# Splitting the first activation tiles in another order, and two unused product groups fewer, in a hybrid attention/SSD layer

## The reference, cut to what matters

```python
h = rms_norm(x, norm_gain[i])                 # x: 1024 x 1024
proj = h @ w_in[i]
q, k, v, z_a, z_s, xbc, dt_raw, gate_pre = jnp.split(proj, offsets, axis=-1)
# attention over q, k, v;  SSD over xbc, dt;  gates;  two projections, merge, output projection
x = x + merged @ w_out[i]
```

## Time and profile before

| | |
|---|---|
| median of 3 runs | 1331.56 us (1331.45 to 1332.23) |
| profiled execution, its own time | 1331.9 us |
| its span in the trace | 1330.1 us |
| PE busy | 1322.8 us, 99% of the span |
| DVE, ACT, POOL busy | 865.2, 638.9, 567.4 us |
| granted PE clock, mean | 1.00 of full speed |

### The profile page before, as it was taken

The page is one execution under the profiler, slowest core; times in us unless marked ns, Lnnn a source line. Parts: engine busy times, 40 slices in busy tenths (PEclk is TensorE's granted clock), DMA queues, the critical chain, the costliest instruction groups (busy, mean ns, idle before and its releaser), DMA issues.

```text
span 1330.1 us, 20357 instructions
## 1 busy us (share of the span) xinstructions
PE 1322.8 (99%) x7018; PEld 1061.8 (80%) x7018; DVE 865.2 (65%) x1051; ACT 638.9 (48%) x1194; POOL 567.4 (43%) x340
## 2 busy tenths in 40 slices
PE   8999999999999999999999999999999999999999
PEld 7878777888888888778788787887888878788887
DVE  7858767766776423567576676665756554377897
ACT  7565354554454333545365364552657554522331
POOL 5644564554454454344233343343145545344300
PEclk9999999999999999999999999999999999999999
DMA  7434564434333322766646666466485455523615
GB/s 221 179 103 131 145 164 145 136 104 126 95 109 112 126 95 89 273 211 203 222 147 221 222 200 221 173 205 224 142 312 213 150 194 198 208 96 142 225 45 190
DMA packets 124608, 223.28 MB, mean 168 GB/s; under 512 B 7650, under 2 KB 84194, under 8 KB 121235
## 3 DMA queue, kind: packets, MB, share of 16 engines
q1 hardware_dynamic: 59586, 174.22, 39.2%
q10 hardware_dynamic: 64880, 48.37, 11.4%
q0 software_dynamic: 96, 0.13, 0.0%
HBM read 154.15 MB, written 63.31 MB: 163 GB/s over the span
## 4 chain that ended last, share of the span: by engine, by line
PE 96%; DVE 1%; DMA 1%; SPq 1%; ACT 1%; issue 0%; DVEq 0%
PE F L199 38%; PE F L1119 37%; PE M L2270 4%; PE M L1322 2%; PE M L1366 2%; PE F L2270 2%; PE F L1360 1%; PE F L1336 1%; PE F L1353 1%; PE F L1063 1%; PE M L1360 1%; PE M L1353 1%; PE F L2224 1%; DMA sb_early<-x 1%; PE M L1315 1%; PE M L1347 1%
## 5 line engine op out<-in xcount | busy, mean ns | idle before, releaser
L1119 PE MATMUL F<-sb_tv,sb_whl 128*128 128x512 f32 x1200 | 287.9, 395 | 0.0
L199 PE MATMUL F<-sb_xb,sb_whl 128*128 128x512 f32 x1152 | 282.9, 402 | 0.0
L1119 PEld LDWEIGHTS F<-sb_tv,sb_whl 128*128 128x128 f32 x1200 | 224.9, 187 | 55.1
L199 PEld LDWEIGHTS F<-sb_xb,sb_whl 128*128 128x128 f32 x1152 | 214.1, 188 | 57.0 <-issue 8.1
L199 PE MATMUL F<-sb_X,sb_whl 128*128 128x512 f32 x1080 | 253.0, 395 | 0.0
L199 PEld LDWEIGHTS F<-sb_X,sb_whl 128*128 128x128 f32 x1080 | 202.3, 187 | 50.1 <-issue 0.5
L482 POOL TENSOR_TENSOR sb_whl<-sb_acc,sb_whl 128x512 fp32r<-128x512 f32 x123 | 172.7, 1412 | 156.6 <-ACT sb_whl L556 156.6
L211 POOL TENSOR_TENSOR sb_whl<-sb_wst,sb_whl 128x1024 fp32r<-128x1024 f32 x50 | 125.8, 2515 | 223.8 <-ACT sb_whl L208 223.7
L1119 PE MATMUL F<-sb_xb,sb_whl 128*128 128x512 f32 x900 | 219.7, 396 | 0.0
L1119 PEld LDWEIGHTS F<-sb_xb,sb_whl 128*128 128x128 f32 x900 | 168.2, 187 | 44.4 <-issue 2.2
L556 ACT ACTIVATE sb_whl<-sb_acc 128x512 fp32r<-128x512 f32 x123 | 76.0, 627 | 98.7 <-PE F L1119 82.0
(11 more groups left out here) (248 smaller groups left out, 1823.3 us busy)
## 6 DMA issues: line engine op xcount, KB each, us to landing
sb_wst<-w_units SPq DMA_DIRECT2D x52, 512.0 KB, 5.2
sb_acc<-cs_d SPq DMA_DIRECT2D x8, 2048.0 KB, 7.2
sb_wst<-w_units SPq DMA_DIRECT2D x14, 1024.0 KB, 4.8
sb_acc<-w_units SPq DMA_DIRECT2D x12, 1024.0 KB, 5.1
x_d<-sb_res ACTq DMA_DIRECT2D x24, 512.0 KB, 3.2
sb_early<-x_d SPq DMA_DIRECT2D x8, 1024.0 KB, 6.3
sb_acc<-ecs_d SPq DMA_DIRECT2D x16, 512.0 KB, 8.2
g_d<-sb_res ACTq DMA_DIRECT2D x16, 512.0 KB, 6.1
```

What stands on the lines that cost most here:

```text
L199: last = nc.tensor.matmul(bank, weight(slot, wp, k), act(ap, k, half), start=(k == 0 and wp == 0 and ap == 0), stop=(k == NK - 1 and wp == 1))
L1119: last = nc.tensor.matmul(F[:, BANK[what], :], ring(idx, wp)[:, k * P:(k + 1) * P], moving(what, ap, k), start=(idx < 4 and k == 0 and wp ...
```

## The change

On ACT, `x_high(0)` moves ahead of `square_x(2)`, `b12_copy(0)` moves behind the high part of v_0, and the high part of dt goes away. On POOL, the high part of dt is new, ahead of the low parts. On DVE, `x_low(0)` moves ahead of `norm_x(2)`. On PE, one of the two first unused products and all four ahead of the vdt products go away; the waits follow the producers.

```diff
@@ POOL
+            pool.wait_ge(v_in1, 32)
+            nc.gpsimd.tensor_copy(vw[:, 0, :, 2 * P:VD], dtraw[:]).then_inc(pads_set, 1)
             pool.wait_ge(v_hi, 1)
             v_low(0)
             pool.wait_ge(dt_lo, 1)
             v_low(1)
-            pool.wait_ge(v_hi, 2)
+            pool.wait_ge(pads_set, 3)
             nc.gpsimd.tensor_tensor(vw[:, 1, :, 2 * P:VD], dtraw[:], vw[:, 0, :, 2 * P:VD].bitcast(f32), ALU.subtract).then_inc(dt_lo, 1)
@@ ACT
             square_x(0)
             square_x(1)
+            x_high(0)
             square_x(2)
-            x_high(0)
             x_high(1)
-            b12_copy(0)
             act.wait_ge(v_in1, 32)
             nc.scalar.activation(v_part(0, 0), raw_v(0), ACT.Copy).then_inc(v_hi, 1)
-            nc.scalar.activation(vw[:, 0, :, 2 * P:VD], dtraw[:], ACT.Copy).then_inc(v_hi, 1)
+            b12_copy(0)
             square_x(3)
@@ DVE
             norm_x(1)
+            x_low(0)
             norm_x(2)
-            x_low(0)
             dve.wait_ge(v_in1, 32)
             nc.vector.tensor_copy(v_part(0, 1), raw_v(1)).then_inc(dt_lo, 1)
             x_low(1)
@@ PE
-            unused_products(2, zpad[:, 0:P], zpad[:])
+            unused_products(1, zpad[:, 0:P], zpad[:])
@@ PE
             transpose_x(0)
             transpose_x(1)
-            unused_products(4, C('ones'), C('ident', 0, 2 * P))
-            pe.wait_ge(v_hi, 2)
+            pe.wait_ge(v_hi, 1)
+            pe.wait_ge(pads_set, 3)
             pe.wait_ge(dt_lo, 1)
```

## The result

The changed kernel takes 1333.72 us (median of 20 runs, 1332.76 to 1334.44) against 1331.53 us (20 runs, 1331.38 to 1332.84): ratio 1.0015, 95% interval 1.0009 to 1.0021, 2.2 us slower. The forecast of 1331.7 us was wrong, and the range of 1330.7 to 1333.4 too short by 0.3 us.

What follows compares the result with a forecast made beforehand. Early pace was set by x tile 3's DMA at 16.01 us, then ACT and DVE, with PE only from 29.54. Terms 0 + 0 + 0.05 + about 0.05 gave 1331.56 + 0.1 = 1331.7 us, range 1330.7 to 1333.4.

Steps and rivals of the forecast that it cites:

- I take it that it does, since nothing here shows a fall: PE ahead of the vdt products: the upper clock level survives a pause of 2.9 us, so no time lost.
- rival 2: PE falls to 1.2 GHz in the pause, slowing the 32 vdt products; 1333.1 or 1336.6 us, chances 0.07 and 0.06.
- recovering form: PE's clock falls in the pause but recovers half way through the vdt products: about +1.5 us, 1333.1, chance 0.07.
- lasting form: PE's clock stays low over all 32 vdt products, taking up to 9.1 us: +5 us, 1336.6, chance 0.06.
- Taking them away gives 0 as long as the vdt products start at about 14.3: PE's four unused products, 11.26 to 13.24, lie wholly in a wait for ACT's dt copy: removal priced 0.
- ACT, POOL and DVE: Reordered early stage: tile 0's high part 0.46 us earlier, tile 1's low part +1.08, POOL copy price 0.
- The start of the vdt products: On PE, DVE's cast of v_1 becomes the last gate: start at 14.37 against 14.32, +0.05 us.
- The slack: Idle margin behind the vdt products, absorbing their +0.05 us later start; some 0.5 us ahead of tile 2's transposes.
- the sum: Unused products 0, POOL 0, vdt start 0.05, high part of tile 3 about 0.05: 0.0 to 0.1 us.
- rival 1: DVE's delay, from tile 1's low part waiting for the pair 0 copy, isn't absorbed: up to +1.1 us, 1332.7, chance 0.12.
- Tile 3 at 16.01: The DMA of x tile 3 lands at 16.01 us and sets the early pace; ACT idles 1.76 us for it.
- -1.25 from below: Bound on the gain: PE's whole idle time from behind 14.32 up to 29.54, 1.25 us.

Runs made afterwards that it cites:

- the run without the four: Kernel before with only the four unused products ahead of the vdt products removed; 1333.20 us, ratio 1.0012.
- the run of the order alone: Changed kernel with both groups of unused products put back (2 and 4), leaving the new order on ACT, DVE and POOL; 1331.94 us, ratio 1.0003.
- half of the filling: Kernel before with two of its four unused products left ahead of the vdt products; median 1331.67 us, ratio 1.0004.

## Why the prediction was wrong

**The step that failed is the clock.** I wrote "I take it that it does, since nothing here shows a fall": the absence of a fall in a trace without such a pause was taken for evidence. The clock's loss was rival 2, with the right cost (the first vdt products at 1.2 GHz) and the right sign (the 32 products over 5 us), and had 0.13 of the chance where it should have had most of it: all three traces of the changed kernel show products at the lower level (6.45, 6.61 and 6.83 us for the 32), and all 20 of its runs (1332.76 and up) are slower than all those 87 of before (1332.56 at most). Its picture was half of what happens. It let PE fall in the pause; that is the trace of the run without the four. In the three traces of the changed kernel the clock had not risen yet when the pause began (422 to 428 ns for the transposes ahead of it, and no fall in the granted clock), and it rose only at about the middle of the vdt products. With the four put back, a clock that was late rose while they ran (3.11 us instead of 1.98), ahead of the vdt products. Its recovering form was priced at 1333.1 and its lasting form at 1336.6; measured was 1333.7, between. The lasting form was priced too high besides: sixteen transposes at 3.63 against twice 1.04 us is a factor of 1.75 and not 2, which makes 7.9 us and not 9.1 of the 4.53. The rule that the prediction cited from the Trainium skill ("TensorE: Matmul & The Clock Gate", Part 1) named the case: by that rule work lifts the clock and idling gives it back. The traces agree in that, with 0.54 of the clock from 14.9 to 18.1 us after a pause of 2.85 us, and in the changed kernel with records of 442 ns up to 19 us, when the vdt products had run since 15.08, and of 297 ns from 19.8 on.

**"Taking them away gives 0 as long as the vdt products start at about 14.3"** was the price of the four products, read from their place in a wait. Their time is free; what they do to the clock is not. Measured: 1.7 us alone.

**ACT, POOL and DVE** came out as worked: in the run of the order alone, high part of tile 0 at 9.88 (9.80 forecast), the cast of v_1 starting at 13.70 (13.63), the low part of tile 1 at 14.71 (14.60), the last norm before the low part of tile 2 ending at 20.08 + 1.28 = 21.36 (21.4). The POOL copy took 0.40 us, inside the bounds of 0 and 0.72.

**The start of the vdt products** was mis-sized: I put 0.06 us between the end of the last producer and PE, as ACT's row had it (14.26 to 14.32). Behind DVE's cast it was 14.64 - (13.70 + 0.69) = 0.25 us. The slack was mis-sized too: ACT's squares waited for a landing at 16.01 in the trace that I took it from, and at 15.67 in that of the order alone, so that ACT wants the high part of tile 2 some 0.3 us earlier. With both, the transposes of tile 2 end when ACT wants them, not 0.4 earlier, and the order costs 0.4 us by the medians instead of the 0.1 of the sum. This is rival 1's time in part; how much of it is the later vdt start and how much the copy of pair 0 is open, as said above.

**"Tile 3 at 16.01"** was right as a pace and wrong as a name. The wait counts the loads of tiles 3 and 4 on one semaphore, so the later of the two set it; with its own, tile 3's square started at 14.02 and 14.15, and tile 4's at 15.98. That the pace lies there held: 0.8 us of earlier vdt start gave nothing.

The bound "-1.25 from below" was never tested by the change. The range failed by its upper end: it took in the recovering clock's middle and not its spread up to 1334.4.

## What to carry to other kernels

Products that nobody reads are not free to remove because they lie in a wait: ask what PE's pause becomes without them, whether the clock has risen when it begins, and what runs behind it. If the trace of before has no such pause, it says nothing on the clock's answer, and the case with the slower products deserves the larger chance. Look at the runs as heaps and at their mean clocks, not at the median alone: half of the filling showed no loss by the median and had it in five runs of eleven. And there is a bound on the other side: six products in place of four bought nothing that can be told.

## What the runs showed of the hardware that I had not expected

- By the granted clock, the level did not fall in the pause but at its end (no record lies in the pause to test it by): in the run without the four it reads 1.00 from 11.5 to 14.2 us, when no product ran, 0.70 from 14.3 to 14.7, and 0.54 from 14.9 to 18.1.
- The point of the rise varies between executions of almost the same start. Four unused products took 1.98 us in one trace and 3.11 in another, though they began at 11.26 in both. With the pause filled, that made no difference to the total that can be told (1331.9 us with the early rise, 1331.63 with the late one).
- The granted clock reads 1.00 ahead of the first recorded change, even where records of 421 to 442 ns show the lower level. Durations of one shape tell it; the column doesn't.
- PE started 0.25 us after the end of a DVE cast, and 0.06 us after the end of an ACT copy, both the last gate of the same products; two more traces of each have 0.26 and 0.26, and 0.05 and 0.05. Why was not tried.
